# A two-block transformer kernel on one core: first loads in pieces, expert slots refilled in finer parts, late tile transposes, roots ahead of casts

## What is computed

```python
for i in range(2):
    m = even_mixer(x, ...) if i % 2 == 0 else odd_mixer(x, ...)
    x = layer_norm(DN_ALPHA * x + m, ln1_g[i], ln1_b[i])
    f = hier_moe(x, ...)              # 32 experts, top 2 of one group of 8, w1, w3: 1024x512, w2: 512x1024
    x = layer_norm(DN_ALPHA * x + f, ln2_g[i], ln2_b[i])
# second block
u = rms_norm_2(h, norm1_gain)
proj = u @ w_in                       # 1024 x 3072, then a linear recurrence and a retention
h = h + mixed @ w_out
u = rms_norm_2(h, norm2_gain)
h = h + (gelu(a) * v) @ ffn_down_w    # up 1024 x 6144 with a convolution over tokens, down 3072 x 1024
return rms_norm_2(h, final_norm_gain)
```

## Time and profile before

| | |
|---|---|
| runs | 1538.03 us median of 3 (1535.84 to 1539.27) |
| profiled execution | 1538.82 us, its span 1537.0 us |
| TensorE | 97% of the span busy |
| VectorE, ScalarE, GpSimd | 36%, 30%, 10% |
| chain that ended last | TensorE 89%, VectorE 4%, DMA 2%, no engine named 2%, ScalarE 2% |
| DMA | 502.66 MB, mean 327 GB/s, 426 to 429 GB/s over most of both expert layers |
| mean granted clock of TensorE | 0.994 of full |

### The profile page before, as it was taken

How to read it: one execution, slowest core, us unless ns; L and a number is a source line. 1 busy time by engine, 2 the same in 40 slices (tenths; PEclk the granted TensorE clock), 3 DMA queues, 4 the chain that set the end, 5 groups by cost and what they waited for, 6 DMA issues and landing times.

```text
span 1537.0 us, 19061 instructions
## 1 busy us (share of the span) xinstructions
PE 1484.3 (97%) x7702; PEld 876.9 (57%) x7702; DVE 546.1 (36%) x1134; ACT 454.0 (30%) x791; POOL 149.6 (10%) x124
## 2 busy tenths in 40 slices
PE   7989999999999999999999999999989999999998
PEld 6765454544534445975554544445434696788886
DVE  5655111111111114035311111211111477588965
ACT  4541111111111112453111111111110571577654
POOL 0211000000000002952100000000000430001200
PEclk9999999999999999999999999999999999999999
DMA  8555899999999999745699999999999765555410
GB/s 297 226 239 219 351 419 429 427 428 428 428 426 429 427 422 402 261 164 230 254 412 426 427 428 427 427 429 428 426 428 408 275 219 193 190 192 192 165 55 28
DMA packets 72850, 502.66 MB, mean 327 GB/s; under 512 B 4416, under 2 KB 5696, under 8 KB 45248
## 3 DMA queue, kind: packets, MB, share of 16 engines
q1 hardware_dynamic: 71904, 495.17, 79.1%
q0 software_dynamic: 864, 6.29, 1.0%
HBM read 500.40 MB, written 1.05 MB: 326 GB/s over the span
## 4 chain that ended last, share of the span: by engine, by line
PE 89%; DVE 4%; DMA 2%; issue 2%; ACT 2%; POOL 0%; SPq 0%; DVEq 0%; ACTq 0%
PE bank L946 29%; PE bank L979 14%; PE bank L805 10%; PE bank L892 8%; PE bank L1250 6%; PE bank L770 5%; PE bank L1278 4%; PE bank L906 3%; PE bank L1252 3%; DMA ring<-in_w_in 1%; DVE X L1731 1%; PE bank L961 1%; PE bank L852 1%; DMA ring<-in_w_qkv 1%; PE bank L864 1%
## 5 line engine op out<-in xcount | busy, mean ns | idle before, releaser
L946 PE MATMUL bank<-ring,arena 128*64 128x512 f32 x1280 | 280.0, 593 | 5.9 <-issue 5.9
L946 PEld LDWEIGHTS bank<-ring,arena 128*64 128x64 f32 x1280 | 93.7, 137 | 187.2 <-issue 187.2
L946 PE MATMUL bank<-arena 128*64 128x512 f32 x576 | 174.8, 611 | 9.1 <-issue 9.1
L1860 DVE TENSOR_TENSOR arena<-arena,bank 128x512 f32<-128x512 f32 x32 | 22.0, 687 | 384.9 <-PE bank L946 384.9
L979 PE MATMUL bank<-ring,arena 128*64 128x512 f32 x640 | 141.7, 595 | 2.4 <-ACT arena L1407 2.4
L1250 PE MATMUL bank<-x_split,w_high 128*128 128x512 f32 (+1 forms) x408 | 139.1, 392 | 0.2 <-DVE x_split L1685 0.2
L892 PEld LDWEIGHTS bank<-SEL,x_by_row 128*128 128x128 f32 x1024 | 116.7, 192 | 25.8 <-issue 24.3
L946 PEld LDWEIGHTS bank<-arena 128*64 128x64 f32 x576 | 57.0, 141 | 121.3 <-issue 121.3
L892 PE MATMUL bank<-SEL,x_by_row 128*128 128x128 f32 x1024 | 122.8, 278 | 0.0
L1874 DVE SCALAR_TENSOR_TENSOR y_low<-bank,ST,y_high 128x512 fp32r<-128x512 f32 x64 | 48.0, 751 | 202.5 <-ACT y_high L1411 202.5
L1411 ACT ACTIVATE y_high<-bank,ST 128x512 fp32r<-128x512 f32 x64 | 44.0, 687 | 245.7 <-PE bank L979 245.7
(11 more groups left out here) (324 smaller groups left out, 2215.4 us busy)
## 6 DMA issues: line engine op xcount, KB each, us to landing
ring<-in_w_gate SPq DMA_DIRECT2D x36, 2048.0 KB, 26.6
ring<-in_w_up SPq DMA_DIRECT2D x32, 2048.0 KB, 24.2
ring<-in_w_down SPq DMA_DIRECT2D x32, 2048.0 KB, 26.0
arena<-in_w_gate SPq DMA_DIRECT2D x18, 2048.0 KB, 26.5
arena<-in_w_up SPq DMA_DIRECT2D x18, 2048.0 KB, 25.5
arena<-in_w_down SPq DMA_DIRECT2D x18, 2048.0 KB, 28.2
ring<-in_ffn_up SPq DMA_DIRECT2D x12, 2048.0 KB, 8.0
ring<-in_w_in SPq DMA_DIRECT2D x9, 2048.0 KB, 14.1
```

The costliest lines, as they stand in the source:

```text
L946: last = nc.tensor.matmul(bank[4 + m][64 * e:64 * e + 64, :], XG[:, c, 64 * e:64 * e + 64], w[e][:, c, :], start=(c == 0), stop=(c == C - 1))
```

## The change

It has these parts, all in one program:

- **First loads.** KT first, then x in two token tiles, then the first weight item in three pieces: rows of tile 0, of tile 1, of tiles 2 and 3. TensorE transposes token tile 0 as soon as KT and its half of x are there. ScalarE waits for the piece that it casts. Borrowed semaphores count the pieces (table2_loaded, bias_loaded, early_loaded), and their later waits are raised by as much.
- **Late transposes.** Before the first expert layer, token tile 0 is transposed after the whole projection instead of before its last group; ScalarE copies both halves of that tile (`evac_whole_token`), VectorE none.
- **Finer first refills.** TensorE raises part_used after steps 0, 1 and 3 of the first gate, step 3 of the first up, and steps 0 and 1 of the first down, whose column halves now alternate step by step. SyncE refills in matching parts; matrices 12 and 13 are new among them.
- **Last down by columns.** The second half of the last pair's down matrices comes in two halves of columns, and TensorE waits for each.
- **Roots ahead of casts.** After an expert layer ScalarE takes the root before it casts weight tiles; an additional small root follows the layer's last silu; GpSimd starts its low tiles only after token tile 0 is normed (x_ready).

```diff
@@ -452,7 +452,8 @@
-        in_parts, PARTS = (POOL, POOL + 1, POOL + 4, POOL + 5), 8
+        in_parts, FIRST_PARTS, USED_PARTS = range(POOL, POOL + 6), 12, 6
+        PARTS = FIRST_PARTS + 2
...
@@ -497,8 +498,9 @@
         def _(sp):
-            sp.dma_start(X[:, :, :], x.rearrange("(t p) d -> p t d", p=P)).then_inc(x_loaded, 16)
             sp.dma_start(KT[:, :], table).then_inc(x_loaded, 16)
+            sp.dma_start(X[:, 0, :], x[0:P, :]).then_inc(x_loaded, 16)
+            sp.dma_start(X[:, 1, :], x[P:SEQ, :]).then_inc(table2_loaded, 16)
...
@@ -523,16 +525,26 @@
                     if n == POOL:
-                        sp.wait_ge(part_used, 3 * l + 1)
+                        sp.wait_ge(part_used, USED_PARTS * l + 1)
+                        load_part(l, n, 0, SLOT // 8)
+                        load_part(l, n + 1, 0, SLOT // 8)
+                        sp.wait_ge(part_used, USED_PARTS * l + 2)
+                        load_part(l, n, SLOT // 8, SLOT // 4)
+                        load_part(l, n + 1, SLOT // 8, SLOT // 4)
+                        sp.wait_ge(part_used, USED_PARTS * l + 3)
+                        load_part(l, n, SLOT // 4, SLOT // 2)
+                        load_part(l, n + 1, SLOT // 4, SLOT // 2)
+                    if n == POOL + 2:
+                        sp.wait_ge(part_used, USED_PARTS * l + 4)
+                        load_part(l, n, 0, SLOT // 2)
+                        load_part(l, n + 1, 0, SLOT // 2)
+                    if n == POOL + 4:
+                        sp.wait_ge(part_used, USED_PARTS * l + 5)
                         load_part(l, n, 0, SLOT // 4)
                         load_part(l, n + 1, 0, SLOT // 4)
-                        sp.wait_ge(part_used, 3 * l + 2)
+                        sp.wait_ge(part_used, USED_PARTS * l + 6)
                         load_part(l, n, SLOT // 4, SLOT // 2)
                         load_part(l, n + 1, SLOT // 4, SLOT // 2)
-                    if n == POOL + 4:
-                        sp.wait_ge(part_used, 3 * l + 3)
-                        load_part(l, n, 0, SLOT // 2)
-                        load_part(l, n + 1, 0, SLOT // 2)
                     if n >= POOL:
...
@@ -555,12 +567,20 @@
                     for words, loaded in ((slice(0, SLOT // 2), first_half), (slice(SLOT // 2, SLOT), None)):
+                        if m == 2 and loaded is None:
+                            continue
                         for k in (2 * m, 2 * m + 1):
...
                                 .then_inc(slot_loaded[slot_no] if loaded is None else loaded, 16)
+                for half in range(2):
+                    for k in (4, 5):
+                        slot_no = ring_item(l, k) % RING
+                        to, src = (a[:, SLOT // 2:SLOT].rearrange("p (j f) -> p j f", f=D)[:, :, 512 * half:512 * half + 512]
+                                   for a in (ring[:, slot_no, :], expert_source(l, EXPERTS - 2 + k % 2, k)))
+                        sp.dma_start(to, src).then_inc(slot_loaded[slot_no] if half else early_loaded[0], 16)
...
@@ -570,9 +590,14 @@
+            src, view = items[I_EIN[0]][0:2]
+            sp.dma_start(view[:, 0:2, :], src[:, 0:2, :]).then_inc(bias_loaded, 16)
+            sp.dma_start(view[:, 2:4, :], src[:, 2:4, :]).then_inc(early_loaded[EARLY - 1], 16)
+            sp.dma_start(view[:, 4:8, :], src[:, 4:8, :]).then_inc(slot_loaded[0], 16)
             for i in I_EIN:
-                load(i)
-                if i == 0:
+                if i != I_EIN[0]:
+                    load(i)
+                else:
                     sp.dma_start(COLS[:, :], cols).then_inc(const_loaded, 16)
...
@@ -657,9 +682,8 @@
             next_norm_rows(0, 1)
-            low_tiles(S_QKV, range(2))
             pool.wait_ge(x_ready, 3)
-            low_tiles(S_QKV, range(2, 3 * TILES))
+            low_tiles(S_QKV, range(3 * TILES))
             pool.wait_ge(x_ready, 4)
...
@@ -924,7 +947,7 @@
-                        first_rows=None):
+                        first_rows=None, columns_ready=None):
...
@@ -946,7 +969,7 @@
                                                     start=(c == 0), stop=(c == C - 1))
-                        if up_free is not None and m == 0 and c in (1, 3):
+                        if up_free is not None and c in ((0, 1, 3), (3,))[m]:
                             last.then_inc(part_used, 1)
...
@@ -983,15 +1006,19 @@
                 if up_free is not None or first_rows is not None:
-                    for half, free in ((0, s["xg_lo"]), (1, s["xg_hi"])):
-                        if next_pair:
-                            pe.wait_ge(free, g + 2)
-                        last = down(half, range(FE // P // 2))
-                    if up_free is not None:
-                        last.then_inc(part_used, 1)
-                    else:
-                        w = [matrix(4), matrix(5)]
+                    for j in range(FE // P // 2):
+                        for half, free in ((0, s["xg_lo"]), (1, s["xg_hi"])):
+                            if next_pair and j == 0:
+                                pe.wait_ge(free, g + 2)
+                            last = down(half, [j])
+                        if up_free is not None:
+                            last.then_inc(part_used, 1)
                     for half in range(2):
+                        if first_rows is not None:
+                            if half:
+                                w = [matrix(4), matrix(5)]
+                            else:
+                                pe.wait_ge(*columns_ready)
                         down(half, range(FE // P // 2, FE // P)).then_inc(s["y_done"], 1)
...
@@ -1048,10 +1075,11 @@
-                            pe.wait_ge(parts_loaded, 16 * (PARTS * l + 6))
+                            pe.wait_ge(parts_loaded, 16 * (PARTS * l + FIRST_PARTS))
...
-                    pe.wait_ge(early_loaded[place - RING], 16 * (6 * AHEAD // POOL * l + turn + 1))
+                    extra = 2 * l if place == RING else 1 if place == POOL - 1 else 0
+                    pe.wait_ge(early_loaded[place - RING], 16 * (6 * AHEAD // POOL * l + turn + 1 + extra))
...
@@ -1068,7 +1096,8 @@
                         next_pair=False,
-                        first_rows=first_halves)
+                        first_rows=first_halves,
+                        columns_ready=(early_loaded[0], 16 * (6 * AHEAD // POOL + 2) * (l + 1)))
                 scatter_by_half(n)
...
@@ -1084,7 +1113,9 @@
             pe.wait_ge(x_loaded, 32)
-            transposes_by_token("x", X)
+            transposes_by_token("x", X, tiles=[0])
+            pe.wait_ge(table2_loaded, 16)
+            transposes_by_token("x", X, tiles=[1])
             keep_clock(3, 3)
...
@@ -1174,7 +1205,9 @@
             transposed("ao")
-            project_out(G_EO, I_EO, range(A_HEADS), first=A_HEADS, final=A_HEADS - 1, beside=lambda: transposes_by_token("ln0", X, x_ready, 0, [0]))
+            project_out(G_EO, I_EO, range(A_HEADS), first=A_HEADS, final=A_HEADS - 1)
+            transposes_by_token("ln0", X, x_ready, 0, [0])
+            pe.wait_ge(pj_free[1], G_EO + 1)
             moe_layer(0, "ln0")
...
@@ -1324,6 +1357,14 @@
+            def evac_whole_token(name, t):
+
+                for h, copied in enumerate((tr_act, tr_dve)):
+                    k = TR[name][0] + 2 * t + h
+                    act.wait_ge(tr_done, k + 1)
+                    src = bank[4 + k % 4][:, :].rearrange("p (c s) -> p c s", s=P)
+                    nc.scalar.copy(XT[:, 4 * h:4 * h + 4, t * P:(t + 1) * P], src).then_inc(copied, 1)
+
             def high_input(name, t, gain=None):
...
@@ -1399,6 +1440,8 @@
                     .then_inc(s["silu_done"], 1)
+                if not next_pair:
+                    nc.scalar.activation(root_warm, rms_eps, ACT.Sqrt)
                 if next_pair:
...
@@ -1439,7 +1482,10 @@
                     i, src, (high, _) = split_tile(s, k)
-                    act.wait_ge(*arrived(i))
+                    if s is S_EIN and k < 2:
+                        act.wait_ge(((bias_loaded, early_loaded[EARLY - 1])[k]), 16)
+                    else:
+                        act.wait_ge(*arrived(i))
                     if k >= TILES or s["free"] is not None:
...
@@ -1515,16 +1561,16 @@
             evac_transposes("ao", lambda b, n: MT[:, b:b + n, :])
-            for t in range(T):
-                norm_root(t)
-                evac_token("ln0", t)
+            norm_root(0)
+            evac_whole_token("ln0", 0)
+            norm_root(1)
+            evac_token("ln0", 1)
             moe_layer(0)
...
-            high_tiles(S_QKV, range(2))
             for t in range(T):
...
                 if t == 0:
-                    high_tiles(S_QKV, range(2, TILES))
+                    high_tiles(S_QKV, range(TILES))
                 high_input("ln1", t)
...
@@ -1536,11 +1582,11 @@
             moe_layer(1)
+            norm_root(0)
             high_tiles(S_IN2, range(2))
-            norm_root(0)
```

(2 more changed lines are left out.)

15 lines of the change are left out of this document (7 added, 8 removed).

## The result

The changed kernel takes **1530.33 us** (median of 5 runs, 1529.24 to 1531.67), the kernel before beside it 1538.38 (5 runs, 1535.84 to 1539.30): ratio 0.9947, 95% interval 0.9936 to 0.9957, 8.1 us less. The forecast was 1532.4, a range of 1528.6 to 1535.8, and faster with a chance of 0.82.

What follows compares the result with a forecast made beforehand. TensorE was taken as most of the chain, the weight stream as ending expert layers, short chains as holding stage borders and first weights the start; -2.9 - 0.2 - 0.4 + 0.2 - 0.4 - 1.9 = -5.6 us gave 1532.4, range 1528.6 to 1535.8.

Steps and rivals of the forecast that it cites:

- First loads: Kernel start: first weight product at 11.65 us, 2.9 us sooner; bounds 0 and 4.1.
- the second half of x lands at 6.5: Kernel start: x's second half lands at 6.5 us, with the table and half of x loaded ahead of it.
- Late transposes: Before the first expert layer: 0.2 us gained, bounds 0 and 0.5, from a 0.23 us TensorE wait.
- 135.2, where the projection ended before: Before the first router product: projection end 133.2 plus 1.97 us from transpose to router gives 135.2, nothing gained there.
- Finer first refills: Expert layers: the early half of the next gate pair gains 0.4 us a layer; bounds 0 and 2.0.
- I cost this edit at nothing: Start of expert layers: refilling the slot part freed after the first step gains 0, since SyncE waits for the flag first.
- the last waits are on the stream: End of expert layers: TensorE waits for the stream of weights, so the refills' gain goes on to the layer's end.
- First border: After the first expert layer: 0.2 us lost, TensorE waiting for the fourth low tile; bounds 2.1 gained, 2.5 lost.
- Second border: After the second expert layer: tile 0's norm 2.15 us sooner, low tiles in time, 1.9 us gained; bounds 0 and 2.2.
- The start's rival: Kernel start: the small first loads land no sooner because pieces travel side by side; 1535.3 us, chance 0.10.
- The lead of the stream lasts: Expert layers: the refills gain 2.0 us a layer instead of 0.4; 1529.2 us, chance 0.12.
- The clock: Rival: one fall of the clock more or less behind a wait, about 1.8 us; 1534.2 or 1530.6 us, chance 0.12.

Runs made afterwards that it cites:

- gate half: Kernel before plus only the early half of the next gate pair (matrices 12 and 13) from the finer refills: 1537.09 us, ratio 0.9994.
- small pieces: Kernel before plus only the smaller refills of down matrices 10, 11 and up matrices 14, 15: 1538.44 us, ratio 1.0006.
- early low tiles: Kernel before plus the border edits, but GpSimd takes two low tiles before token tile 0 is normed: 1535.21 us, one run.
- refills alone: Kernel before plus only the finer first refills (new load_part blocks and part_used counts): 1536.99 us, ratio 0.9993.

## Why the prediction was right, and where its terms were off

- **What bounds the kernel**: right. In all 28 layers the end follows how far the stream is, and a late fall of the clock is taken up by the wait for it.
- **First loads**: the mechanism right, the term mis-sized, 2.9 against 2.09 in this profile and about 2.0 over seven. The step that failed is "the second half of x lands at 6.5", from bytes over rate. The first of sixteen signals is there at 6.0; the last comes 0.7 to 2.4 later. That ScalarE's casts and not the transfer set the first cast was right, as was the absence of a gap at the second item.
- **Late transposes**: 0.2 against 0.78, outside its own bound of 0.5. The step that failed is "135.2, where the projection ended before", which took an estimate of 133.2 and a rounded copy for exact.
- **Finer first refills**: 0.4 a layer against 1.54 and 1.07 in this profile, 1.06 over 18 layers. The gate half wins and loses as told, and alone it ends with nothing. Two steps failed. "I cost this edit at nothing", of the small pieces: alone they show nothing clear of noise, but with the gate half 0.26 MB stay, 0.6 us a layer. The forecast had its 0.4 from the gate half by itself, which keeps nothing, so that 0.4 lies near 0.6 is luck. And "the last waits are on the stream" was taken as bytes alone, while the length goes with the spread of the sixteen signals too, some 0.5 us a layer.
- **Last down by columns**: 0, right.
- **First border**: +0.2 against +0.26 up to the same product of the windowed attention, right; 4 x 2.35 plus one blocked stretch of 1.0 (forecast 1.1), and TensorE waits for the fourth low tile. The loss is GpSimd's late start: with early low tiles this border gains 0.5.
- **Second border**: -1.9 against -1.86 by TensorE's later marks; the first product comes 2.15 sooner behind the last down, less 0.3 in the waits behind it. The slower scaling of tile 1 wasn't foreseen, nor did it matter.
- **Rivals**: VectorE wasn't starved. The start's rival (no sooner at all) fell, though the start was the term with a loss. "The lead of the stream lasts" was half right. The clock fell once less in layer 0, and it gave little there: inside a layer the wait for the stream takes up a fall (0.08 us, standard error 0.10, for a late one), where the prediction priced it at 1.8. Outside it cost 1.2 to 1.7, and 2.2 in the one profile that has it within a border.

## What to carry to other kernels

A wait for a DMA ends with the last of sixteen signals. Here bytes over rate gave 6.5 us for x's second half, 0.3 to 0.6 behind its first signal and 0.2 to 1.9 ahead of its last: leave a us or two for the last. Where buffers limit a stream, a lead won early is spent at the next place where they run out, so look for that place before counting it; and judge an edit inside such a stage by the stage's length over several layers and profiles, since a launch hides 1 us. Keeping GpSimd's long element-wise work away from the VectorE instruction that everybody waits for made that instruction end 1.8 us sooner, six times what the order of the roots gave. But ask what waits for GpSimd's work as well: at the second border TensorE gained all of the 1.8, at the first it lost 0.7.

## What the runs showed beside that

TensorE's pace in the wide up projection has two values from one execution to the next, at full granted clock in both: from its first to its last product 139.9 us in eight profiles and 137.5 in six, before and after the change both 139.9. TensorE's groups of that stage (mean ns of one), 1360 to 1460 us, kernel before and refills alone:

```profile
L1250 PE MATMUL bank<-x_split,w_high 128*128 128x512 f32 x284 | 100.4, 399 | 0.0
L1252 PE MATMUL bank<-x_split,w_low 128*128 128x256 f32 x283 | 79.5, 281 | 0.0
```

```profile
L1262 PE MATMUL bank<-x_split,w_high 128*128 128x512 f32 x285 | 98.8, 394 | 0.0
L1264 PE MATMUL bank<-x_split,w_low 128*128 128x256 f32 x285 | 78.9, 277 | 0.0
```

What picks the pace is open. With the falls of the clock it could be much of the scatter between launches; timed runs have no trace to show it. Five of the fourteen profiles have a fall at 74 to 76 us, in the attention, and begin expert layer 0 1.4 to 1.7 us late for it, counted from the first product. Windows of the run with the gate half alone; the third number from the end is the granted clock, 0.57 here and 1.00 in the kernel before:

```profile
75.00:79.00 4.00, 3.62 (x19) 3.59 (x20) 0.94 (x3) 2.20 (x10) 0.00 (x0) 0.57 1.05 446
```
